# Sliding attention's scores with the keys' two parts stacked over 128 rows, two passes a head instead of three

## The reference

```python
q, k, v = jnp.split(h @ w_qkv, [Hq * d, Hq * d + Hkv * d], axis=-1)   # Hq = 16, Hkv = 4, d = 64
q = apply_rope(q.reshape(B, S, Hq, d), cos, sin).reshape(B, nb, L, Hkv, G, d)
k = apply_rope(k.reshape(B, S, Hkv, d), cos, sin)
...
s = jnp.einsum('bnqhgd,bnchd->bnhgqc', q, kb).astype(jnp.float32) * (d ** -0.5)
...
mask = (jnp.abs(kpos - qpos) <= WINDOW) & (kpos >= 0) & (kpos < S)
```

## Time and profile before

| | |
|---|---|
| median of three runs | 1955.87 us |
| profiled execution: its own time, its span | 1958.0 us, 1955.7 us |
| PE busy | 1923.1 us, 98% |
| DVE, ACT, POOL busy | 1188.4, 922.6, 1127.4 us |
| sliding attention, first score group to the turn after the last one | 1395.13 to 1511.79 us of the span |

### The profile page before, as it was taken

One profiled execution on the slowest core, in us unless ns is written; L12 is line 12 of the kernel. 1 busy time (PEld: TensorE's weight loads), 2 busy tenths in 40 slices (PEclk: granted clock), 3 DMA queues, 4 the chain that ended last, 5 costly groups with the idle time before them and its releaser, 6 DMA issues.

```text
span 1955.7 us, 25037 instructions
## 1 busy us (share of the span) xinstructions
PE 1923.1 (98%) x9072; PEld 1579.4 (81%) x9072; DVE 1188.4 (61%) x1986; ACT 922.6 (47%) x1736; POOL 1127.4 (58%) x856
## 2 busy tenths in 40 slices
PE   8999999999999999999999999999999999999998
PEld 6778888888888887777788888888788888888887
DVE  6773324453432487987774745856588775746755
ACT  5644336533333365664543443445587543433443
POOL 5335454454444457675675666664775576656663
PEclk9999999999999999999999999999999999999999
DMA  4113233233232235545323222323111323222321
GB/s 162 65 61 105 89 115 128 92 113 103 97 111 97 97 108 160 153 132 159 130 93 101 98 89 99 104 96 105 55 44 44 130 97 106 97 89 97 100 94 65
DMA packets 75722, 199.49 MB, mean 102 GB/s; under 512 B 7376, under 2 KB 26192, under 8 KB 75600
## 3 DMA queue, kind: packets, MB, share of 16 engines
q1 hardware_dynamic: 75600, 197.90, 31.0%
HBM read 183.19 MB, written 14.68 MB: 101 GB/s over the span
## 4 chain that ended last, share of the span: by engine, by line
PE 90%; DVE 5%; DMA 2%; issue 1%; ACT 1%; POOL 1%; SPq 1%; DVEq 0%; POOLq 0%; ACTq 0%
PE b L409 28%; PE b L413 28%; PE b L417 28%; PE b L439 2%; PE b L429 1%; DMA turned<-fa 1%; PE b L479 1%; PE b L474 1%; DVE sm L617 1%; DMA ra<-turned 1%; PE b L490 1%; PE b L432 1%; PE b L433 0%; SPq L233 0%; DVE ra L525 0%
## 5 line engine op out<-in xcount | busy, mean ns | idle before, releaser
L253 POOL TENSOR_TENSOR ra<-raw,ra 128x512 fp32r<-128x512 f32 x632 | 876.7, 1395 | 737.5 <-ACT ra L297 735.8
L409 PE MATMUL b<-ra 128*128 128x512 f32 (+1 forms) x2560 | 891.0, 393 | 21.0 <-ACT ra L297 8.3
L413 PE MATMUL b<-ra 128*128 128x512 f32 (+1 forms) x2560 | 878.3, 388 | 0.5 <-DVE ra L670 0.3
L417 PE MATMUL b<-ra 128*128 128x512 f32 (+1 forms) x2560 | 878.4, 388 | 0.0
L297 ACT ACTIVATE ra<-raw 128x512 fp32r<-128x512 f32 x632 | 391.9, 628 | 519.3 <-PE b L417 510.2
L409 PEld LDWEIGHTS b<-ra 128*128 128x128 f32 x2560 | 481.9, 189 | 126.4 <-issue 21.8
L417 PEld LDWEIGHTS b<-ra 128*128 128x128 f32 x2560 | 482.0, 188 | 99.5
L413 PEld LDWEIGHTS b<-ra 128*128 128x128 f32 x2560 | 482.7, 189 | 95.8 <-DVE ra L525 0.9
L786 DVE TENSOR_TENSOR h<-b,h 128x512 f32<-128x512 f32 x136 | 91.6, 682 | 58.2 <-PE b L417 57.7
L677 DVE TENSOR_TENSOR tmp<-b,rb 128x512 f32<-128x512 f32 x66 | 45.0, 688 | 111.7 <-PE b L417 111.5
L677 DVE TENSOR_TENSOR gbuf<-b,rb 128x512 f32<-128x512 f32 x50 | 34.2, 689 | 93.1 <-PE b L417 93.1
(11 more groups left out here) (278 smaller groups left out, 1875.5 us busy)
## 6 DMA issues: line engine op xcount, KB each, us to landing
raw<-in_f_g SPq DMA_DIRECT2D x40, 512.0 KB, 3.4
raw<-in_f_v SPq DMA_DIRECT2D x40, 512.0 KB, 3.4
raw<-in_f_d SPq DMA_DIRECT2D x40, 512.0 KB, 3.4
raw<-in_w_up SPq DMA_DIRECT2D x32, 512.0 KB, 3.4
raw<-in_w_down SPq DMA_DIRECT2D x32, 512.0 KB, 3.4
turned<-fa SPq DMA_DIRECT2D x32, 256.0 KB, 4.3
ra<-turned SPq DMA_DIRECT2D x64, 128.0 KB, 2.8
raw<-in_p_g SPq DMA_DIRECT2D x16, 512.0 KB, 3.5
```

What stands on the lines that cost most here:

```text
L253: e.tensor_tensor(wl, src, wh.bitcast(F), ALU.subtract).then_inc(*w_low.mark(n))
L409: e.matmul(m.banks[b][:, 0:xh.shape[-1]], wh[:, c:c + 128], xh, start=start, stop=False)
L413: e.matmul(m.banks[b][:, 0:xh.shape[-1]], wh[:, c:c + 128], xl, start=False, stop=False)
L417: last = e.matmul(m.banks[b][:, 0:xh.shape[-1]], wl[:, c:c + 128], xh, start=False, stop=stop)
```

## The change

The key tile holds the high parts of a head in one half of the 128 rows and the low parts of the same head in the other half; the query tile of a head holds its high parts twice, in both halves, and its low parts twice in a second plane. A matmul over 128 rows then gives high times (high + low), a second one with the queries' low parts gives low times (high + low). A head's scores are two such passes. The copies between halves of the rows are made by DMA from a staging tile: four transfers of 256 KB for each query tile, four of 128 KB for each key tile, issued by SyncE (`kind == "stack"`). Queries from the third tile on all pass through one staging tile, the place of the rotary tables.

```diff
+        elif kind == "stack":
+            moves, before, stacked = a
+            for t in before:
+                w.wait_ge(*t)
+            for dst, src in moves:
+                e.dma_start(dst, src).then_inc(*stacked.mark(n, 16))
...
+        elif kind == "score_stacked":
+            b, nk, c0, (qh, ql), k, i, lo, free, ready = a
+            for t in free + ready:
+                w.wait_ge(*t)
+            ps = m.banks[b][:, c0:c0 + nk]
+            qs, ks = slice(128 * i, 128 * i + 128), slice(lo, lo + nk)
+            e.matmul(ps, qh[:, qs], k[:, ks], start=True, stop=False)
+            e.matmul(ps, ql[:, qs], k[:, ks], start=False, stop=True).then_inc(*score.mark(n))
...
+        if kind == "score_stacked":
+            return 2 * (0.0133 + a[1] / 2400.0)
...
+    def stacked_rope(key, stage, free, moves, sig, gate=always, eng="p", low="p"):
+        def carry(low_done, read):
+            yield 0, "sp", lambda: (low_done, *read)
+            x = done("sp", sig, row("stack", moves, (low_done, *read), m.sig(sig)))
+            free[stage] = qk_tok[key] = (x,)
...
+            yield 0, "ac", lambda: (g, *free[stage]) if gate() and free[stage] is not None else None
+            before, free[stage], read = free[stage], None, now("pe")
+            def tell(y):
+                T.release(j, y)
+                launch(carry(y, read))
+            yield from parts_of((stage_of(stage)[:, 0, :], stage_of(stage)[:, 1, :]), t1, (g,), low, lambda: before, tell)
...
+        def q_tile(j, gate):
+            stage = OO + 2 + j if j < 2 else "rope"
+            moves = [(m.ra[halves[z], q_slot(2 * j + r), :, :].bitcast(F), stage_of(stage)[halves[r], :, :].bitcast(F)) for r in range(2)
+                     for z in range(2)]
+            return stacked_rope(("q3", j), stage, stage_free, moves, f"stacked{j % 2}", gate)
...
-            yield from linear("s_q", 1, 8, rhs_u, 1, rope_tile(QK + j % 2, ("q3", j), 1.0, gate), lb, first=j)
+            yield from linear("s_q", 1, 8, rhs_u, 1, q_tile(j, gate), lb, first=j)
```

More of the change, by code:

```diff
@@ L1529, in scores @@
                         assert rw == krow
-                        n = row("score", b, nk, c0(i), (qh, ql), rw, (kh, kl), i, lo, bank_free[b] or (),
-                                high_of((*qt, *kt_)), (*qt, *kt_), i == step[0])
+                        if kl is None:
+                            n = row("score_stacked", b, nk, c0(i), (qh, ql), kh, i, lo, bank_free[b] or (),
+                                    (*qt, *kt_))
+                        else:
+                            n = row("score", b, nk, c0(i), (qh, ql), rw, (kh, kl), i, lo, bank_free[b] or (),
+                                    high_of((*qt, *kt_)), (*qt, *kt_), i == step[0])
                         bank_free[b] = None
@@ L1666, in rope_tile, with process, stage_of @@
         return lambda _, b, tok: launch(process(b, tok))
+    def stacked_rope(key, stage, free, moves, sig, gate=always, eng="p", low="p"):
[3 more added lines that the diff above has]
+            free[stage] = qk_tok[key] = (x,)
+        def process(b, tok):
+            yield 0, "v", lambda: (tok, t_cr[0]) if t_cr[0] and len(T.free) >= 5 else None
+            i, sh, f1 = T.get()
+            j, t1, f2 = T.get()
+            n = row("rope", sh, t1, b, tok, cr, sr, eng, f1, f2, t_cr[0])
+            bank_free[b] = (done("ve", "rope_v", (n, 1)),)
+            g = done("ve", "rope_v", n) if eng == "v" else done("gp", "elem_p", n)
+            T.release(i, g)
+            yield 0, "ac", lambda: (g, *free[stage]) if gate() and free[stage] is not None else None
[4 more added lines that the diff above has]
+            yield from parts_of((stage_of(stage)[:, 0, :], stage_of(stage)[:, 1, :]), t1, (g,), low, lambda: before, tell)
+        return lambda _, b, tok: launch(process(b, tok))
+    def stage_of(stage):
+        return rope[:, :, :].bitcast(R) if stage == "rope" else m.ra[:, stage, :, :]
     o_tok = {}
@@ L2350, in kv_of, with q_slot, k_tile @@
             return (t // 2) // 4
+        def q_slot(t):
+            return (OO + 6, QK)[t // 2 % 2] + t % 2
         def Q3(t):
-            j = t // 2
-            return (*hl(QK + j % 2), 64 * (t % 2), qk_tok[("q3", j)]) if ("q3", j) in qk_tok else None
+            return (*hl(q_slot(t)), 0, qk_tok[("q3", t // 2)]) if ("q3", t // 2) in qk_tok else None
         def K3(t):
             g = kv_of(t)
-            return (*hl(KK + g), 64 * (t % 2), qk_tok[("k3", g)]) if ("k3", g) in qk_tok else None
+            return (m.ra[:, KK + g, t % 2, :], None, 0, qk_tok[("k3", g)]) if ("k3", g) in qk_tok else None
+        halves = (slice(0, 64), slice(64, 128))
+        stage_free = {"rope": (), **{OO + z: free0 for z in range(4)}}
+        def k_tile(g, eng):
+            x = stage_of(OO + g)
+            moves = [(m.ra[halves[r if z == 0 else 1 - r], KK + g, r, :].bitcast(F), x[halves[r], z, :].bitcast(F)) for r in range(2)
+                     for z in range(2)]
+            return stacked_rope(("k3", g), OO + g, stage_free, moves, f"stackedk{g}", eng=eng, low="v")
+        def q_tile(j, gate):
+            stage = OO + 2 + j if j < 2 else "rope"
+            moves = [(m.ra[halves[z], q_slot(2 * j + r), :, :].bitcast(F), stage_of(stage)[halves[r], :, :].bitcast(F)) for r in range(2)
+                     for z in range(2)]
+            return stacked_rope(("q3", j), stage, stage_free, moves, f"stacked{j % 2}", gate)
         def V3(t):
@@ L2368, in second_block_sliding @@
         evac_first = [v_tile(u, VV + g, ("v3", g), always) for g in range(2)]
-        evac_first += [rope_tile(KK + g, ("k3", g), free=lambda: free0, eng="pv"[g], low="v") for g in range(2)]
+        evac_first += [k_tile(g, "pv"[g]) for g in range(2)]
         yield from linear("s_first", 4, 8, rhs_u, 4, lambda j, b, t: evac_first[j](0, b, t), LB7)
```

## The result

The changed kernel takes 1963.86 us against 1956.44 before. Of its seven runs one, in a slow state, took 2639.14 us at a granted clock of 0.683; it counts in that median and not in what follows, and the other six took 1960.55 to 1967.34 us (median 1962.83). Their ratio to before is 1.0036, 95% interval 1.0026 to 1.0046, so 5 to 9 us slower. 1955.1 was forecast, with a range up to 1962.0.

What follows compares the result with a forecast made beforehand. It took TensorE to bound sliding attention, VectorE close behind. Groups −7.8, waits for VectorE +6.6 and the start +0.4 gave −0.8 us: 1957.2 for the profiled execution, 1955.1 for the median, range 1948.5 to 1962.

Steps and rivals of the forecast that it cites:

- What bounds the kernel: Sliding attention is bound by TensorE with hardly a margin, so less TensorE work need not be less time.
- The groups: Score groups on TensorE: 0.48 and 0.70 us each, saving 0.27 and 0.22; 7.8 us over 16 of each size.
- Rival 3: Extra 0.39 us lies in starting any score group, not in 64 rows; groups cost 0.87 and 1.09; 1962.4 us, chance 0.08.
- VectorE's need by pair: VectorE needs 14.5 us in pair 3, 13.0 in pairs 4 to 6, 7.4 in pair 7, run at 97%.
- New waits: TensorE waiting for VectorE in pairs 3 to 7: 6.6 us; at pair 0's first scores: 0.4 us.
- The start: Seven more triples ahead of pair 0 bring TensorE to its scores at 1400.0; it stalls 0.4 us for the query tile.
- The transfers: First query tile's four 256 KB transfers land after 6.1 us, between ends of 5.3 and 13.8; later tiles cost nothing.
- Rival 2: The transfers between halves of the rows are late: 8.1 us of stall at the start, 1962.8 us; chance 0.13.
- The clock: Pair 7's waits of about a microsecond could slow some TensorE matmuls; taken as inside the range.
- the sum: −7.8 + 6.6 + 0.4 = −0.8 us over the profiled execution, giving 1955.1 us for the median.

Runs made afterwards that it cites:

- three_passes: The changed kernel with its transfers and order, but each head's scores made by three matmuls on 64 rows, two heads side by side; 1969.53 us.
- plain_one: The changed kernel with pair 0 alone making its scores as before the change, the other seven pairs stacked; 1957.49 us.
- short_belief: The changed kernel with the planner taking a set of four transfers between halves for 1.0 us in place of 5.2; 1965.78 us.
- one_pass: The changed kernel in its written order with one matmul for each head's scores in place of two, queries' low parts left out; 1961.55 us.
- kept_busy: The changed kernel in its written order, with 26 matmuls nobody reads put where TensorE waits longest; 1962.18 us.
- thin_additions: The changed kernel in its written order, with 24 additions to the residual made on one column only; 1960.84 us.

## Why the prediction was wrong

- What bounds the kernel: right. TensorE was the bound with hardly a margin, and a chain with VectorE in it took over.
- The groups: right in kind, somewhat too large in sum. With a triple behind them they save 0.27 and 0.23 us, where 0.27 and 0.22 were forecast; between turns, where half of them stand, 0.22 and 0.17. By three_passes the gain is 5.9 us of TensorE's work, not 7.8; the groups between turns account for a part of the difference, the rest is open.
- Rival 3, that the edge stays: wrong, by the same run; a group takes 0.56, not 0.87.
- VectorE's need by pair: right in size, wrong as a rate. I let it run at 97%; it reached 91%, as the waits are of dependent steps (argued, since no run parts the chain from VectorE's load). New waits in all: 9.5 us, where 6.6 + 0.4 were forecast.
- The start: the landing was right (1400.3, where 1400.4 was forecast), by luck, since the set went out 0.9 us sooner and took 0.8 longer than I had it; and so was the wait for it (0.37 us, where 0.4 was). But I costed the later start beyond that wait at nothing, since the seven triples put ahead of pair 0 are work only moved. With the stretch behind them bound by the chain, the time does not come back: the first group is 5.2 us later, and plain_one, whose first pair needs no transfers, starts as early as before and regains 6.3 of 7.0 (it also changes the order and has no fall of the clock in its profile). In the sum over TensorE the same 5 us appear as waits in pairs 3 to 7.
- The transfers: the first query tile's set takes 6.9 us (1393.38 to 1400.3) against the 6.1 I took. TensorE waits for it only 0.37 us, and still it is dear: it is what keeps the first group back, and the seven triples fill that time. Rival 2 named nearly the time (1962.8) but by a stall of 8.1 us that is not there; where TensorE arrived early (short_belief) it stood still for 7.4 us at two tiles.
- The clock: I put it inside the range at nothing. It is 5.1 us in the profiled execution and about 2 in the median. The rule of the Trainium skill, "TensorE: Matmul & The Clock Gate", section "Part 1: The HAM clock gate", that lack of activity lowers the clock between two levels, is borne out as far as the two levels go: behind the wait at pair 0 of short_belief triples' matmuls start 0.43 us apart, not 0.23. When a wait brings a fall stays open here.

Together, for the profiled execution: −5.9 (groups by three_passes) + 9.5 (waits) + 5.1 (clock) − 0.7 (one triple fewer ahead of the last product) = 8.0 of the 9.7 measured; 1.7 is not assigned. By stretches nothing is left over: 5.2 (the first group is later) − 0.6 (from there to the last product at full clock, 126.6 against 127.2) + 5.1 (clock) = 9.7.

The step that failed is the sum itself. It took TensorE's saving in full (7.8 us, where 5.9 were measured) and three things too low: the new waits at 7.0 us, where 9.5 were measured, the later start beyond its wait at nothing, where 5.2 were lost, and the clock at nothing, where 5.1 were lost. The first two are not to be added: the waits of pairs 3 to 7 hold what the start lost. Behind all three stands one mistake: the stretch had a second bound, the chain with VectorE in it, only about a microsecond below TensorE's.

## What to carry to other kernels

When an engine is 98% busy, measure how far below it the next bound lies before counting a saving: here it was about 1 us in 127, and of some 8 us more taken from TensorE (one_pass) about a third arrived. In this stretch filler work decided mainly where the waits stand; what counted was when the chain begins, so latency in front of its first step was paid in full, even where a planner hid it behind useful work. A wait of the matmul engine of 1.5 to 2.3 us may cost as much again in clock: it did three times in the changed kernel's profile, and not behind the waits of 1.6 us in plain_one's.

## What the runs showed of the hardware

- Four transfers of 256 KB between halves of the rows take 3.9 us to issue, and the last lands 6.9 us after the first went out (first query tile of the changed kernel); one lands after 4.7 to 4.9 us in the middle, where 512 KB from HBM takes 3.4. The changed kernel's transfers by kind (KB each, us to landing):

```profile
ra<-rope SPq DMA_DIRECT2D x24, 256.0 KB, 4.9
ra<-ra SPq DMA_DIRECT2D x8, 256.0 KB, 4.7
```

- Six 64-row matmuls of two heads cost more than four 128-row ones do: 0.27 us more with 256 keys between turns and a triple, 0.17 with 384 between turns. Most of it is the entry: two turns start 0.31 us ahead of a 64-row group and 0.14 ahead of a 128-row one.
- Three times in the changed kernel's profile waits of 1.5 to 2.3 us in all were followed by a stretch at the lower clock, 1.7 us lost each time. In kept_busy, with idle matmuls in the waits (0.8 us at most left of one), none was; nor was the unfilled wait of 2.3 us in thin_additions.
